# One transformer forward in float32: the first adaLN phase by output channels in two halves, with half of the first layer's z products between them

## The reference, cut to what matters

```python
mod_c = (sc @ ada_w[i] + ada_b[i]).reshape(6, D_MODEL)
hc = _rmsnorm(xc, norm_w[i, 0]) * (1.0 + mod_c[1]) + mod_c[0]
...
xz = h @ w_up
x_m, z = xz[..., :ML_D_IN], xz[..., ML_D_IN:]
x_c = jax.nn.silu(_dwconv(x_m, conv_w, conv_b))
...
out = (hn + skip * x_c) * jax.nn.silu(z)
return (out @ w_down, ...)
...
xc = xc + mod_c[2] * oc
```

## Time and profile before

| | us |
|---|---|
| median of 3 runs (lowest to highest) | 1843.75 (1842.93 to 1846.68) |
| the profiled execution, its time | 1840.74 |
| its span, from the first to the last instruction | 1839.1 |
| PE matmuls busy | 1793.7 |
| DVE busy | 1389.5 |
| ACT busy | 1002.4 |
| mean granted PE clock | 0.996 of full |

### The profile page before, as it was taken

One profiled execution on the slowest core, in us unless ns is written; L12 is line 12 of the kernel. 1 busy time (PEld: TensorE's weight loads), 2 busy tenths in 40 slices (PEclk: granted clock), 3 DMA queues, 4 the chain that ended last, 5 costly groups with the idle time before them and its releaser, 6 DMA issues.

```text
span 1839.1 us, 27506 instructions
## 1 busy us (share of the span) xinstructions
PE 1793.7 (98%) x11032; PEld 1494.3 (81%) x11032; DVE 1389.5 (76%) x2140; ACT 1002.4 (55%) x1567; POOL 143.8 (8%) x122
## 2 busy tenths in 40 slices
PE   5999999999999999999999999999999999999998
PEld 3988877797888867888977778888888787878888
DVE  3854777668898767999865698988665877779984
ACT  3744445446674454776354466745653445456753
POOL 1100121000000011000101100001100210010001
PEclk8999999999999999999999999999999999999999
DMA  9565656857665766675674777566555746445552
GB/s 393 211 225 197 203 207 242 307 221 292 261 216 205 288 250 265 252 277 198 216 311 166 298 283 294 204 224 266 207 185 183 240 163 225 171 172 195 197 173 80
DMA packets 74318, 421.27 MB, mean 229 GB/s; under 512 B 12400, under 2 KB 18952, under 8 KB 26576
## 3 DMA queue, kind: packets, MB, share of 16 engines
q1 hardware_dynamic: 56016, 395.68, 57.5%
q10 hardware_dynamic: 18176, 23.85, 4.0%
HBM read 408.51 MB, written 10.96 MB: 228 GB/s over the span
## 4 chain that ended last, share of the span: by engine, by line
PE 86%; DVE 5%; issue 3%; DMA 2%; ACT 2%; POOL 1%; SPq 0%; ACTq 0%; POOLq 0%; DVEq 0%
PE ps L654 17%; PE ps L676 10%; PE ps L711 9%; PE ps L657 9%; PE ps L636 6%; PE ps L692 5%; PE ps L714 5%; PE ps L639 3%; PE ps L622 3%; PE ps L624 3%; PE ps L623 3%; PE ps L755 3%; DMA raw<-in_stream 2%; DVE spl_lo L499 2%; PE ps L962 1%
## 5 line engine op out<-in xcount | busy, mean ns | idle before, releaser
L499 DVE TENSOR_TENSOR spl_lo<-raw,spl_hi 128x1024 fp32r<-128x1024 f32 x556 | 690.0, 1266 | 148.4 <-ACT spl_hi L488 147.1
L488 ACT ACTIVATE spl_hi<-raw 128x1024 fp32r<-128x1024 f32 x556 | 574.2, 1053 | 299.9 <-PE ps L714 109.5
L654 PE MATMUL ps<-H,spl_hi 128*128 128x512 f32 x1408 | 444.4, 397 | 3.7 <-DVE H L1854 2.9
L657 PEld LDWEIGHTS ps<-H,spl_lo 128*128 128x128 f32 x1408 | 264.5, 188 | 62.5
L657 PE MATMUL ps<-H,spl_lo 128*128 128x256 f32 x1408 | 276.7, 278 | 0.0
L654 PEld LDWEIGHTS ps<-H,spl_hi 128*128 128x128 f32 x1408 | 214.3, 189 | 17.9 <-issue 14.2
L711 PE MATMUL ps<-G,spl_hi 128*128 128x512 f32 x528 | 165.8, 395 | 0.0
L636 PE MATMUL ps<-B,spl_hi 128*128 128x512 f32 x512 | 160.8, 395 | 0.0
L622 PE MATMUL ps<-H,spl_hi 128*128 128x256 f32 x512 | 148.3, 290 | 1.8 <-DVE spl_lo L499 1.1
L623 PE MATMUL ps<-H,spl_hi 128*128 128x256 f32 x512 | 145.2, 284 | 0.0
L624 PE MATMUL ps<-H,spl_lo 128*128 128x256 f32 x512 | 145.0, 283 | 0.0
(11 more groups left out here) (251 smaller groups left out, 2927.4 us busy)
## 6 DMA issues: line engine op xcount, KB each, us to landing
raw<-in_stream SPq DMA_DIRECT2D x366, 1024.0 KB, 5.0
out_new_C<-c_stage ACTq DMA_DIRECT2D x16, 512.0 KB, 3.8
column<-in_ada_cols SPq DMA_DIRECT2D x16, 512.0 KB, 5.3
cond_all<-cond_out ACTq DMA_DIRECT2D x3, 1024.0 KB, 7.3
ada_b<-in_ada_b ACTq DMA_DIRECT2D x3, 768.0 KB, 9.1
E<-rows_out ACTq DMA_DIRECT2D x8, 256.0 KB, 4.3
Em<-rows_out ACTq DMA_DIRECT2D x8, 256.0 KB, 4.5
x<-in_x SPq DMA_DIRECT2D x1, 1024.0 KB, 6.7
```

The source lines that it names most:

```text
L488: act.activation(spl_hi[m % SPL][:, :], raw[r % RAW][:, h * HALF:(h + 1) * HALF], ACT.Copy).then_inc(S["hi_done"], 1)
L499: dve.tensor_tensor(spl_lo[m % SPL][:, :], raw[r % RAW][:, h * HALF:(h + 1) * HALF], spl_hi[m % SPL][:, :].bitcast(F32), ALU.subtract).the ...
L654: pe.matmul(banks[:, b * 512:(b + 1) * 512], spl_hi[m % SPL][:, c], H[:, kk * 512:(kk + 1) * 512], start=kk == 0, stop=False, skip_group_c ...
L657: mm = pe.matmul(banks[:, b * 512:b * 512 + TOK], spl_lo[m % SPL][:, c], H[:, kk * 512:kk * 512 + TOK], start=False, stop=kk == KD - 1, sk ...
```

## The change

- The first phase (layer 0, shift and scale of the first norm) is cut by output channels instead of by input rows alone: a tile holds two row blocks of 128, and 512 columns of each of the two vectors, so four tiles (`ADA_HALF`) give shift and scale of channels 0 to 511 and the next four those of 512 to 1023. The bias is no longer added to the sums; it is in `small` as columns and is added in `first_columns`. `first_rows` replaces the transposes: four matmuls with a small 0/1 matrix (`fold`), which also add the two row blocks' sums.
- z tiles 1, 3, 5, 7 of layer 0 become four tiles `z_first`, by half of the input channels and part (two z tiles' 512 columns). `first_gates` computes half 0 with H chunks 0 to 3 between the two groups of adaLN tiles, and half 1 behind them, into the banks `ACC[0]` to `ACC[3]`. ACT makes their silus (`first_silu`) and sends them to a DRAM buffer `z_out`, 1 MB. In the heads of layer 0 each is loaded into `t1[1]` (`z_load`) in place of its product.
- The heads of layer 0 keep z tiles 0, 2, 4, 6, now as `gate_z(2 * h + 2)` ahead of `head_rows(h)`, and none in head 3. All use `UP[0]`.
- Fills: none in the first norm (2 before), 5 before the gates (3 before), 2, 1, 2, 5 in the heads (2, 3, 3, 2 before). `ada_b` of layer 0 is loaded at once behind stream tile 18 instead of in two parts behind tiles 4 and 14.

```diff
-NORM_FILL = {0: (0, 0, 1, 1), **{q: (1, 1, 2, 1) for q in range(1, 2 * DEPTH - 1)}, 1: (0, 1, 3, 1)}
-CONV_FILL = {0: 3, 3: 2}
+NORM_FILL = {0: (0, 0, 0, 0), **{q: (1, 1, 2, 1) for q in range(1, 2 * DEPTH - 1)}, 1: (0, 1, 3, 1)}
+CONV_FILL = {0: 5, 3: 2}
 V_FILL = 1
-HEAD_FILL = {0: [2, 3, 3, 2], 3: [0, 0, 0, 0]}
+HEAD_FILL = {0: [2, 1, 2, 5], 3: [0, 0, 0, 0]}
...
-    fill(ADA_PHASE)
+    for half in range(2):
+        fill(ADA_HALF)
+        order += [("z_first", 0, half, part) for part in range(2)]
...
+            def first_rows(half):
+
+                pe.wait_ge(S["modb_done"], half + 1)
+                for b in range(4):
+                    mm = pe.matmul(ADA_PS[:, 4 * b:4 * b + 4], mod_b[:, b * P:(b + 1) * P], sc("fold", 0, 4),
+                                   start=b == 0, stop=b == 3, skip_group_check=True)
+                mm.then_inc(S["modT_mm"], 1)
+
+            def first_gates(half, part, fills=0, inner=None):
+
+                n = INDEX["z_first", 0, half, part]
+                for h in range(2):
+                    m = 2 * n + h
+                    pe.wait_ge(S["lo_done"], m + 1)
+                    for kk in range(2):
+                        k = 4 * half + 2 * h + kk
+                        if part == 0:
+                            chunk_ready(0, k)
+                        x_hi, x_lo = both_of(H)(k)
+                        for b in range(4):
...
+                            pe.matmul(out, w_hi, x_hi, start=st, stop=False, skip_group_check=True)
+                            pe.matmul(out, w_hi, x_lo, start=False, stop=False, skip_group_check=True)
+                            mm = pe.matmul(out, w_lo, x_hi, start=False, stop=en, skip_group_check=True)
+                        if h == 1 and kk == 0 and inner is not None:
+                            inner()
+                    mm.then_inc(S["half_used"], 1)
+                    if h == 0:
+                        fill(fills)
...
                     fill(HEAD_FILL[i][h])
-                    gate_z(max(1, 2 * h))
+                    if i:
+                        gate_z(max(1, 2 * h))
+                    elif h + 1 < MH:
+                        gate_z(2 * h + 2)
                     head_rows(j, h)
...
-                    if h:
+                    if h and i:
                         gate_z(2 * h + 1)
...
-            fill(ADA_PHASE - 3)
-            mod_rows(0, 0)
+            fill(ADA_HALF - 3)
+            first_rows(0)
+            first_gates(0, 0, 1)
+            fill(2)
+            first_gates(0, 1, 1, lambda: first_rows(1))
+            first_gates(1, 0)
+            first_gates(1, 1)
...
+            def first_silu(part):
+
+                act.wait_ge(S["h_done"], 4)
+                tile_used(act, INDEX["z_first", 0, 1, part])
+                for c in range(2 * part, 2 * part + 2):
+                    act.activation(zs[:, c * 512:(c + 1) * 512], ACC[c][:, :], ACT.Silu).then_inc(S["zs_done"], 1)
+                act.wait_ge(S["zs_done"], 2 * part + 2)
+                act.dma_start(z_out[2 * part:2 * part + 2].rearrange("t p c -> p t c"),
+                              v3(zs[:, part * 1024:(part + 1) * 1024], 512)).then_inc(S["zs_kept"], 16)
...
+                def z_load(t):
+                    act.wait_ge(S["z_mul"], 8 * j + t + 1)
+                    act.dma_start(t1[t % 2][:, :], z_out[t // 2]).then_inc(S["z_loaded"], 16)
...
+                if q == 0:
+                    for half in range(2):
+                        first_columns(half)
+                        for g in range(2 * half, 2 * half + 2):
+                            scale(g)
+                            split_lo(dve, 2 * half, (g % 2,))
+                            h_lo(g)
+                        split_lo(dve, 2 * half + 1)
+                    split_lo(dve, 4)
+                    return
```

More of the change, by code:

```diff
@@ L160, in mod_index @@
 def mod_index(i, phase):
-    return 3 * i + phase - ((i, phase) > (COLUMN_LAYER, 1))
+    return 3 * i + phase + (i + phase > 0) - ((i, phase) > (COLUMN_LAYER, 1))
 def chunked(w, k0, nk, c0, nc):
@@ L206, in host_tile @@
         p, k = divmod(tile[2], ADA_PHASE)
+        if i + p == 0:
+            half, m = divmod(k, ADA_HALF)
+            return np.concatenate([w["ada_w"][0][kk * P:(kk + 1) * P, v * D + 512 * half:v * D + 512 * (half + 1)]
+                                   for kk in (2 * m, 2 * m + 1) for v in MOD_SOURCE[0:2]], 1)
         rows = w["ada_w"][i][k * P:(k + 1) * P]
         return np.concatenate([rows[:, v * D:(v + 1) * D] for v in MOD_SOURCE[2 * p:2 * p + 2]], 1)
+    if kind == "z_first":
+        cols = [w["ml_w_up"][0][:, DIN + 256 * t:DIN + 256 * (t + 1)] for t in (4 * tile[3] + 1, 4 * tile[3] + 3)]
+        return chunked(np.concatenate(cols, 1), 4 * tile[2], 4, 0, 512)
     if kind == "ml_x":
@@ L283, in host_arrays @@
     put("cond", np.stack([columns(w["c_ctx"]), columns(w["c"][0])], 2).reshape(P, 2 * KD))
+    put("ada_first", np.concatenate([columns(w["ada_b"][0].reshape(6, D)[v]) for v in MOD_SOURCE[0:2]], 1))
+    for r in range(4):
+        for c in range(NS):
+            small[32 * r + c, COL["fold"] + NS * (r % 2) + c] = 1.0
     put("ada_c", np.concatenate([columns(w["ada_b"][COLUMN_LAYER].reshape(6, D)[v]) for v in MOD_SOURCE[2:4]], 1))
@@ L1866, in scaled_rows, with scale @@
                                              ALU.mult)
-                for g in range(4):
+                def scale(g):
                     if g >= 2:
```

125 lines of the change are left out of this document (88 added, 37 removed).

## The result

The changed kernel takes **1879.28 us** (median of 4 runs, 1878.09 to 1881.6) against 1843.65 for the kernel before beside it: a ratio of 1.0192, 95% interval 1.0178 to 1.0207, or 35.6 us more. The forecast was 1864.4 with a range of 1853 to 1871. The sign was right, the size not: 20.65 us were foreseen, and the time lies outside the range.

What follows compares the result with a forecast made beforehand. PE (TensorE), full through the first mixer except in an idle start, was taken to bound the kernel. Start to gates +26.0 us and heads -5.35 gave +20.65 on a median of 1843.75: 1864.4 us, range 1853 to 1871.

Steps and rivals of the forecast that it cites:

- The first z product at 27.8: Start: the first z product on H comes at 27.8 us instead of 35.58, 7.8 earlier.
- Step (a): Start: PE waits 2.4 us for the second half of H, and 0.15 at the next chunk.
- The 0.84 us taken off: Start: a wait of 0.84 us on H in the kernel before, caused by its chunk order, goes.
- Step (b): Start: granted clock again 0.50 before the first product; 0.9 us more lost as a z half runs in it.
- Rival 3: Heads: the clock falls in the three longest waits, 1.8 us each, 5.4 in all, giving 1869.8 us; chance 0.18.
- Step (c): Before the gates: the fifth adaLN tile in a row exceeds the ring of four buffers; PE waits 2.2 us.
- Gates to heads, nothing: Between gates and heads: nothing changes, since the four z silus are moved on ACT, not added.
- The heads' waits, 18.05 us: Heads: new PE waits sum to 18.05 us against 23.4 of z tiles removed, so heads get 5.35 shorter.
- The silus: Heads 1 and 2: z products wait 3.9 and 3.3 us for ACT's silu, since all use one bank.
- the C tiles: Values 2 and 3: PE waits 2.5 and 2.45 us for DVE's low half of the C tile.
- the down tile: Start of the down projection: PE waits 3.15 us for DVE's first split, which z tile 7 covered before.
- Behind the heads, nothing: From the down projection on: nothing changes and PE's own work rules again.

Runs made afterwards that it cites:

- e6: Changed kernel with 70 products of unread result keeping PE busy in three of its new waits, no wait shortened: 1873.98 us, ratio 1.0161.
- e1: Changed kernel with the first layer's head fills of adaLN tiles back at 2, 3, 3, 2 instead of 2, 1, 2, 5: 1869.7 us, ratio 1.0133.
- e3: Changed kernel with ACT's silu of z tiles 2, 4 and 6 ahead of the load, state copies and query work: 1875.59 us, ratio 1.0169.
- e4: Changed kernel with DVE's low part of the next C tile and first down tile ahead of the head's columns: 1875.68 us, ratio 1.0163.
- e14: Changed kernel plus e1, e3, e4, two adaLN tiles back ahead of the x tiles, two start-order edits and 8 small start products: 1852.77 us, ratio 1.0042.
- the halves alone: Kernel before with only the first adaLN phase in halves, no z products between, first x tile's splits behind H's first half: 1849.19 us, ratio 1.003.

## Why the prediction was wrong

- **The first z product at 27.8**: 28.63, right to a microsecond in this execution; 28.8 to 31.1 in six others of the same start.
- **Step (a)**, 2.4 + 0.15 for the second half of H: 2.31, right. The 0.84 us taken off beside it were misread. The row is of the weight load (PEld), and PE's adaLN products ran meanwhile:

```profile
39.05 0.19 PEld L622 LDWEIGHTS ps<-H,spl_hi 128*128 128x128 f32 x1 [0.84 <-DVE H L1854]
```

From the first product on H to the gates PE was idle for 0.78 us in all. In the changed kernel it is 6.55, which is 5.77 more, and the three new waits of 2.31, 2.89 and 0.56 sum to 5.76: no old wait has gone.
- **Step (b), the clock, at 0.9 us in the start and at nothing in the heads and behind them: this is the step that failed.** It is the only place where the sum of the forecast has the clock at all. The same products took 16.5 us longer: some 5 in the start, some 5 in the heads, 5.9 behind them and 0.8 between. The forecast was short by 15. Rival 3 had the mechanism, at three falls of 1.8 us. Its price per fall had no row behind it: the start of the kernel before has not one stretch of 3.7 us at half speed but two, of 3.4 from 20.5 and 6.8 from 30.7. And a fall costs by what PE has to do in it: the one from 399.3 has PE busy for 10.1 of 13.7 us, so about 5 us. That the clock costs time and not the waits alone, e6 shows: 5.7 us came back with the waits filled and not shortened.
- **Step (c)**, 2.2 us for the fifth adaLN tile before the gates: 2.89 + 0.56, and the mechanism was another. It was the *fourth* tile that came late. In the stream the first qk tile stands ahead of the row, so of the four buffers it holds one, which the fourth adaLN tile takes; DVE made that qk tile's low part only by 111.9, after the last x product. I had counted the ring from the row's own first tile. In head 3 the count was right: there it is the fifth that comes late.
- **Gates to heads, nothing**: +0.8 us, right.
- **The heads' waits, 18.05 us**: 16.0 of PE idle. The silus 2.58 and 1.72 with 0.6 to 0.7 moved to the state copies (forecast 3.9 and 3.3), the C tiles 1.99 each (2.5 and 2.45), the landing 3.67 (2.75), the down tile 2.76 (3.15). All the mechanisms are there, each to about a microsecond and most of them smaller than forecast, and e1, e3 and e4 took each away by its own cause. The heads still got only 2.1 us shorter instead of 5.35, by 4.5 us of clock and 0.8 that the z tiles weigh less there.
- **Behind the heads, nothing**: failed, +6.5. The clock stays at 0.50 until 413.0, from the row of five adaLN tiles on, and falls twice more far behind. Idle time there grew by 0.6.
- **The idle time as a whole** was forecast as 0.8 up to the gates (26.0 less 23.4 of z tiles, 0.9 of small matmuls and 0.9 of clock) and 18.05 in the heads, 18.85, and measured as 20.9. The reading of the waits was sound, but that the totals come so near is in part luck: up to the gates it was 4.3 instead of 0.8, in the heads 2.05 less than forecast. The range was too narrow because its upper end took three falls with one landing, when the forecast itself had eight new waits of 2 to 4 us.

No version here beats the kernel before. The best with z products in the start, e14, is 0.42% slower [0.3, 0.55], the halves alone 0.3% [0.2, 0.39]. By e14's profile the start comes out even: the gates are 24.4 us later, for 23.4 of moved z tiles and 0.9 of small matmuls, although the first product comes 5.5 us earlier. The heads keep 5.0 us of waits (L833, DVE's copy of the modulation rows, 2.8; the state copies 2.2), and the stretch behind them is 2.0 longer. So moving the z products won at best what the halves cost, and the waits in the heads are the loss that stays. Whether another order on DVE and ACT would take those away too wasn't tried.

## What to carry to other kernels

Where one engine is full, cost a new wait twice: its length, and the work behind it at the clock that it leaves. Here 20.9 us of new idle time came with 16.5 us of longer products. Filling a gap with moved work pays only if the place that it leaves needs no cover: here four z tiles covered two silus, three splits and a landing. And of a row of prefetched tiles, ask which buffer each one takes and who holds it now, not only how many buffers there are.

## What the hardware showed that I had not expected

- Falls of the granted clock after short waits: to 0.50 at 51.2 us in the changed kernel, 0.9 behind a wait of 2.31 us, and at 385.7, 1.0 behind one of 1.99.
- 70 useless products in three waits made the kernel 5.7 us faster by keeping the clock, although PE is the engine that bounds it.
- The 8,890 records of the same products behind the down projection's start take 1437.3 us of PE or 1443.3. Some 3.4 us of that difference are two falls of the clock, over 660 us behind the last edited instruction.
